# Attention rounds of a hybrid decoder kernel: exponential, turn and product put one, two and three steps behind the scores

## What is computed

```python
def swa_prompt(q, k, v, sinks):            # window attention of the prompt
    ...
    s = jnp.einsum('bnqkgd,bnskd->bnkgqs', qb, kk) * SW_HEAD_DIM ** -0.5
    ...
    p = sink_softmax(jnp.where(mask, s, NEG), sinks)
    o = jnp.einsum('bnkgqs,bnskd->bnqkgd', p, vv)

def mem_attend(cq, mk, mv, q_norm):        # memory attention, prompt and samples
    q = head_rms(cq.reshape(B, L, MEM_HEADS, MEM_HEAD_DIM), q_norm)
    s = jnp.einsum('blhd,bmhd->bhlm', q, mk.astype(F32)) * MEM_HEAD_DIM ** -0.5
    p = jax.nn.softmax(s, axis=-1)
    return jnp.einsum('bhlm,bmhd->blhd', p, mv.astype(F32)).reshape(B, L, MEM_WIDTH)
```

## Time and profile before

| | us |
|---|---|
| median of 3 runs | 3210.73 (3206.9 to 3217.41) |
| the profiled execution | 3207.76 |
| its span, first to last instruction | 3206.0 |
| TensorE busy | 2960.2 (92%) |
| VectorE, ScalarE, GpSimd busy | 1284.7, 694.7, 640.7 |
| mean granted TensorE clock | 0.938 of full |

### The profile page before, as it was taken

One profiled execution on the slowest core, in us unless ns is written; L12 is line 12 of the kernel. 1 busy time (PEld: TensorE's weight loads), 2 busy tenths in 40 slices (PEclk: granted clock), 3 DMA queues, 4 the chain that ended last, 5 costly groups with the idle time before them and its releaser, 6 DMA issues.

```text
span 3206.0 us, 42285 instructions
## 1 busy us (share of the span) xinstructions
PE 2960.2 (92%) x16482; PEld 2630.6 (82%) x16482; DVE 1284.7 (40%) x2195; ACT 694.7 (22%) x1164; POOL 640.7 (20%) x322
## 2 busy tenths in 40 slices
PE   6899999998899999999978878979789999999999
PEld 5678888887799999999966765767569999999997
DVE  4223444444444444444462223233353444444444
ACT  4321122222211111111143313333332111111110
POOL 4003232223312111221140010000023112211220
PEclk9889999999899999999988789798779999999999
DMA  4011011111111111121111210001002111211111
GB/s 157 20 53 44 25 40 47 47 34 41 40 40 46 53 39 39 40 58 39 39 47 33 73 27 14 14 14 43 14 14 60 39 39 44 54 39 39 39 46 54
DMA packets 186027, 135.37 MB, mean 42 GB/s; under 512 B 19616, under 2 KB 175456, under 8 KB 185888
## 3 DMA queue, kind: packets, MB, share of 16 engines
q1 hardware_dynamic: 181760, 129.69, 14.5%
q10 hardware_dynamic: 4160, 4.19, 0.4%
HBM read 124.61 MB, written 11.27 MB: 42 GB/s over the span
## 4 chain that ended last, share of the span: by engine, by line
PE 80%; DVE 6%; PEld 5%; ACT 4%; issue 3%; POOL 1%; PEldq 1%; DMA 0%; ACTq 0%; SPq 0%; DVEq 0%
PE ps L1366 41%; PE ps L1403 22%; PE ps L1528 3%; PEld ps L1366 3%; PE ps L1553 3%; PEld ps L1671 2%; PE ps L1538 1%; PE ps L1392 1%; PE ps L1618 1%; ACT prob L633 1%; POOL w_lo L509 1%; PE ps L1584 1%; DVE x L940 1%; ACT w_hi L505 1%; DVE normed_gained L937 1%
## 5 line engine op out<-in xcount | busy, mean ns | idle before, releaser
L937 DVE TENSOR_TENSOR x<-x,ps 128x512 f32<-128x512 f32 (+1 forms) x882 | 604.6, 686 | 919.0 <-PE ps L1403 913.7
L509 POOL TENSOR_TENSOR w_lo<-w_raw,w_hi 128x1024 fp32r<-128x1024 f32 x194 | 465.3, 2417 | 2302.6 <-ACT w_hi L505 2302.6
L1366 PE MATMUL ps<-hT_hi,w_hi 128*128 128x352 f32 x2976 | 724.7, 333 | 23.7 <-POOL w_lo L509 21.3
L1366 PE MATMUL ps<-hT_lo,w_hi 128*128 128x352 f32 x2976 | 715.4, 328 | 0.1
L1366 PE MATMUL ps<-hT_hi,w_lo 128*128 128x352 f32 x2976 | 708.6, 327 | 0.0
L1366 PEld LDWEIGHTS ps<-hT_hi,w_hi 128*128 128x128 f32 x2976 | 524.4, 192 | 61.7 <-issue 23.2
L1366 PEld LDWEIGHTS ps<-hT_lo,w_hi 128*128 128x128 f32 x2976 | 525.7, 192 | 35.3 <-issue 7.5
L1366 PEld LDWEIGHTS ps<-hT_hi,w_lo 128*128 128x128 f32 x2976 | 525.3, 191 | 26.5 <-issue 1.3
L1403 PE MATMUL ps<-w_hi,m_hi 128*128 128x512 f32 (+1 forms) x1072 | 439.9, 410 | 20.6 <-POOL w_lo L509 8.8
L1403 PE MATMUL ps<-w_lo,m_hi 128*128 128x512 f32 (+1 forms) x1072 | 432.4, 403 | 0.0
L1403 PE MATMUL ps<-w_hi,m_lo 128*128 128x512 f32 (+1 forms) x1072 | 430.8, 402 | 0.0
(11 more groups left out here) (220 smaller groups left out, 2584.5 us busy)
## 6 DMA issues: line engine op xcount, KB each, us to landing
w_raw<-in_w_ffn_in_dram SPq DMA_DIRECT2D x176, 256.0 KB, 3.2
w_raw<-in_w_ffn_out_dram SPq DMA_DIRECT2D x88, 256.0 KB, 3.7
w_raw<-in_w_in_hgrn_dram SPq DMA_DIRECT2D x52, 256.0 KB, 4.6
w_raw<-in_w_out_dram SPq DMA_DIRECT2D x32, 256.0 KB, 3.7
w_raw<-in_w_in_swa_dram SPq DMA_DIRECT2D x24, 256.0 KB, 4.1
x<-in_x_prompt_dram SPq DMA_DIRECT2D x8, 512.0 KB, 9.4
w_raw<-in_w_mem_kv_dram SPq DMA_DIRECT2D x16, 256.0 KB, 5.7
cache<-in_cache_mem_k_dram SPq DMA_DIRECT2D x4, 1024.0 KB, 7.2
```

What stands on the lines that cost most here:

```text
L509: nc.gpsimd.tensor_tensor(slot(1, s), raw[:, j3, :], slot(0, s).bitcast(F32), ALU.subtract).then_inc(w_lo, 1)
L937: return V_.tensor_tensor(out, a, b, op)
L1366: return mmul(ps[:, b0 + g, 0:TW], slot(a, s)[:, P * k:P * k + P], hT[b][:, k, TW * g:TW * g + TW], start=m < 3, stop=m >= 69)
```

## The change

ACT: the exponential moves one step back (round s-1 in step s), `prompt_hi` to the end of the step and one round forward (even steps from 4), the hook `after` goes. DVE: `prompt_lo` likewise, between the two halves of `second`, which is now called twice; the sample portions move behind the maximum. PE: each step begins with rows, turn and scores; the first filler, the sample portions, `prompt_out` of the same step's round s-3 and the second filler follow. `STEPS` goes from 20 to 19, and the projections, sums and roots for the next queries move one step forward, with 12 instead of 9 matmuls in a half. One wait is added at step 3.

```diff
--- before.py
+++ after.py
@@ -139,7 +139,7 @@
 
 B_SC, B_PT, B_RO, B_SS, B_F = 0, 2, 3, 4, 5
 
-ROUNDS, STEPS = 16, 20
+ROUNDS, STEPS = 16, 19
 S_KT, S_SSC, S_SPT, S_SPV, S_SOUT = 4, 5, 15, 17, 18
 
 INIT = 6
@@ -684,27 +684,25 @@
                                                sample_rows(rr, h2), ACT.Copy)
                 ins.then_inc(oA.sem, 1)
 
-            def pair(p, g, before, after=None):
+            def pair(p, g, before):
 
                 for s in range(STEPS):
                     before(s)
-                    if s >= 5 and s % 2:
-                        prompt_hi(p, (s - 5) // 2)
                     if s == S_SOUT:
                         sample_hi(p)
                     if s == S_SSC + NB:
                         sample_exp(p, None if g is None else col(S_SROW + g))
                     if 2 <= s < ROUNDS + 2:
                         prompt_turn(ROUNDS * p + s - 2)
-                    if s < ROUNDS:
-                        half, _, h2 = at_round(s)
-                        prompt_exp(ROUNDS * p + s, None if g is None else col(S_SINK + 3 * (2 * half + h2) + g))
+                    if 1 <= s < ROUNDS + 1:
+                        half, _, h2 = at_round(s - 1)
+                        prompt_exp(ROUNDS * p + s - 1, None if g is None else col(S_SINK + 3 * (2 * half + h2) + g))
                     if S_KT <= s < S_KT + NB:
                         sample_turn(p, s - S_KT, 2 if g is None else 1)
                     if s == S_KT + NB and g is None:
                         sample_values(p)
-                    if after:
-                        after(s)
+                    if s >= 4 and s % 2 == 0:
+                        prompt_hi(p, (s - 4) // 2)
 
             def ffn(L):
                 def split(jb, it, s, extra):
@@ -856,10 +854,10 @@
                             if g < QG - 1:
                                 if s == 11:
                                     pump.upto(n0 + 4)
-                                if s == 15:
+                                if s == 14:
                                     head_squares(u + 2, B_F)
                                     pump.upto(n0 + 5)
-                                if s == 16:
+                                if s == 15:
                                     query_std(u + 2, B_F)
                             elif s == 11:
                                 pump.upto(n0 + 4)
@@ -1121,14 +1119,10 @@
             def pair(p, g, first, second=None, s_blocks=0):
                 for s in range(STEPS):
                     first(s)
-                    if s >= 5 and s % 2:
-                        prompt_lo(p, (s - 5) // 2)
                     if s == S_SOUT:
                         sample_lo(p)
                     if s == S_SSC + NB + 1:
                         sample_scale(p, g)
-                    if s == S_SPT + 1:
-                        sample_turn(p, g)
                     if 3 <= s < ROUNDS + 3:
                         prompt_rows(ROUNDS * p + s - 3)
                     if 2 <= s < ROUNDS + 2:
@@ -1138,10 +1132,16 @@
                         prompt_max(ROUNDS * p + s, None if g is None else 3 * (2 * half + h2) + g)
                     if s == s_blocks:
                         sample_blocks()
+                    if second:
+                        second(s, 0)
+                    if s == S_SPT:
+                        sample_turn(p, g)
+                    if s >= 4 and s % 2 == 0:
+                        prompt_lo(p, (s - 4) // 2)
+                    if second:
+                        second(s, 1)
                     if s == S_SSC + NB - 1:
                         sample_max(p, g)
-                    if second:
-                        second(s)
 
             def hgrn_head(h):
                 if h == 0:
@@ -1338,17 +1338,15 @@
                             if g and s == 3:
                                 query_norm(u + 1)
                                 wait(dve, qN, u + 1, "n")
-                            if 1 <= s <= NT:
-                                add_group(G0 + 2 * s - 2, s - 1, 0)
-                            if g < QG - 1 and s == 15:
+                            if g < QG - 1 and s == 14:
                                 head_gain(u + 2, B_F, qh[:, 0, :], col(S_GQ))
                             if g < QG - 1 and s == 16:
                                 wait(dve, aE, r0 + 7, "exp")
                                 query_norm(u + 2)
 
-                        def second(s, G0=G0):
+                        def second(s, n, G0=G0):
                             if 1 <= s <= NT:
-                                add_group(G0 + 2 * s - 1, s - 1, 1)
+                                add_group(G0 + 2 * s - 2 + n, s - 1, n)
 
                         pair(2 + g, g, first, second, 3 if g else 0)
                 ffn(L)
@@ -1624,14 +1622,9 @@
 
                 for s in range(STEPS):
                     r = ROUNDS * p + s
-                    if s >= 5 and s % 2:
-                        prompt_out(r - 4)
-                    if S_SSC <= s < S_SSC + NB:
-                        sample_scores(p, s - S_SSC, window)
-                    if s == S_SPV:
-                        sample_rows_mm(p, window)
-                    fill(s, 0)
                     if 3 <= s < ROUNDS + 3:
+                        if s == 3 and p > 2:
+                            wait(pe, oV, p - 1, "7")
                         if s >= 5:
                             wait(pe, oV, p, f"{(s - 5) // 2}")
                         prompt_rows(r - 3, window)
@@ -1643,11 +1636,18 @@
                         prompt_turn(r - 2)
                     if s < ROUNDS:
                         prompt_scores(r, window)
-                    fill(s, 1)
+                    fill(s, 0)
+                    if S_SSC <= s < S_SSC + NB:
+                        sample_scores(p, s - S_SSC, window)
                     if S_KT <= s < S_KT + NB:
                         sample_keys(p, s - S_KT, 1 if window else 2)
                     if s == S_SPT:
                         sample_turn(p, window)
+                    if s == S_SPV:
+                        sample_rows_mm(p, window)
+                    if s >= 4 and s % 2 == 0:
+                        prompt_out(r - 3)
+                    fill(s, 1)
 
             def hgrn_head(h, j):
                 inc = hT_.sem
@@ -1909,14 +1909,14 @@
                             if s == 11 and z == 0:
                                 pe.wait_ge(x_added, (o + 1) * OUTG)
                                 wait(pe, qD, u + 1, "std")
-                            if 11 <= s < 15:
-                                feat(J + 2, 0, B_F, qP, (2 * (s - 11) + z, 8))
-                            if s == 15 and z == 1:
+                            if 11 <= s < 14:
+                                feat(J + 2, 0, B_F, qP, (2 * (s - 11) + z, 6))
+                            if s == 14 and z == 1:
                                 query_sums(u + 2, B_F)
-                            if s == 17 and z == 0:
+                            if s == 16 and z == 0:
                                 wait(pe, qD, u + 2, "std")
-                            if s >= 17:
-                                feat(J + 3, 1, B_F, qP, (2 * (s - 17) + z, 6))
+                            if s >= 16:
+                                feat(J + 3, 1, B_F, qP, (2 * (s - 16) + z, 6))
 
                         if g:
                             wait(pe, qN, u, "n")
```

## The result

The changed kernel takes 3089.7 us (median of 4 runs, 3087.6 to 3093.5) against 3211.4 us before: a ratio of 0.962, with a 95% interval of 0.960 to 0.964. The forecast was 3089 us. Its profiled run has a span of 3085.8 us, 120.2 us less than before.

The account below looks back on a forecast made before the run. TensorE was taken to bound the kernel, losing time in and around the five attention pairs. Gains of 18 + 18 + 31 + 31 + 24 = 122 us took 3210.7 to 3089 us; 8-in-10 range 3055 to 3150 us.

Parts of the forecast that it names:

- pair 4: Last window pair: gain 24 us; nine unfilled steps from step 10, kept at low clock, take 57 us against 62.7.
- outside the pairs: Everything outside the five attention pairs, some 2519 us: not touched by the diff, so no gain.
- The steady steps: Window-pair steps with filler: 6.3 us each; five take 31.4 us, against 40.5 in pair 3 and 45.6 in pair 4.
- signs named in advance: Trace marks of a right forecast, among them five window-pair steps in 31 to 33 us and no exp wait for the maximum.
- k_cacheT gone: In sample_scores, PE's waits for the copied transposed cache keys disappear; they were 11.0 us in eight waits of one window pair.
- The rival in which the clock stays up everywhere: Denser steps keep the clock up from step 10: 38 us more gain, 18 of it in pair 4; 3051 us; chance 0.09.
- From step 10 in pairs 2 and 3: Rest of these window pairs from step 10: 76.3 us falls to 58.4 us, gain 18 us in each.
- slower rival: Out waits for DVE's rows of the same step, 3.29 us every even step: 132 us lost, 3221 us; chance 0.06.
- The start of the window pairs: Scores(1) runs inside the w_lo chain and step 4 loses waits: gain 4 us in each of three pairs.
- Memory pairs: Pairs 0 and 1: gain 18 us each; in pair 0, 5.3 from steps 4 to 7 and 8 from steps 8 to 10.
- Wait and clock: Split of the whole gain: some 88 us from removed waits and 34 us from a higher clock.
- The 19 steps: Loop cut from twenty steps, with one more wait at step 3, already met by then: no effect.

Follow-up runs that it names:

- rows first: The changed kernel with DVE's prompt_rows moved ahead of the head gain and the sample scale: 3094.3 us, ratio 0.964.
- split first: The changed kernel with the w_lo split of step 0 moved ahead of the squares of the next head: 3091.4 us, ratio 0.963.

## Why the prediction was right

The total is right to 1 us, but its terms were not that good; the misses cancel. In us, gain forecast and measured:

| part | forecast | measured |
|---|---|---|
| pair 0 | 18 | 11.9 |
| pair 1 | 18 | 12.1 |
| pair 2 | 31 | 28.6 |
| pair 3 | 31 | 24.7 |
| pair 4 | 24 | 37.9 |
| outside the pairs | 0 | 5.0 |
| sum | 122 | 120.2 |

*The steady steps* were rebuilt well: 31.4 us for five, measured 32.6 in pairs 3 and 4; memory steps 4 to 7 21.8 us, measured 23.3. In the fed step shown above the halves of the filler cost 1.59 and 1.48 us for the 1.5 and 1.4 of the forecast, and rows 0.84 for 0.75: that is the miss of 0.2 to 0.4 us a step. The step of before was read rightly, and most signs named in advance came: k_cacheT gone, exp right behind the copy, five steps in 31 to 33 us, clock at 1.00 in the fed steps. One did not: the clock was to stay at 1.00 until the sample rows of pairs 2 and 3. In pair 3 these start at 2118 us, and the mean from 2101 to 2111 us was 0.51.

*Pair 4* is the large miss, 14 us too low. The forecast kept the low clock for its bare steps "as they hold it now"; the term that failed is this one, 57 us for the rest of the pair, measured 42 from the rows of step 10. The clock went into step 10 at 1.00, out of five steps without a wait (in the earlier trace rows they had 0.81), and it stayed there to 2220 us, past waits of 0.9 to 1.4 us. The rival in which the clock stays up everywhere was nearly right in this one place: 18 us more in pair 4, measured 14. How long it stays up is in part luck: in the kernels with rows first and with the split first it fell 74 and 80 us behind the pair's first scores, not 88, and the pair was 2 to 3 us longer.

*From step 10 in pairs 2 and 3*, 58.4 us was forecast and 67.1 us stand in pair 3 from the rows of step 10 (65.6 from its scores, above). The terms most mis-sized, from rows to rows, are step 14, which was to take 4.5 us and took 8.0, step 15 (5.2 for 3.1) and steps 11 and 16 (9.4 for 7.7 and 7.0 for 5.3); the mean clock from 2101 to 2111 us, in steps 14 to 16, was 0.51. The rows of step 14:

```profile
2094.99 1.32 DVE L1000 TENSOR_SCALAR q_heads<-ps,params 128x1056 f32<-128x1056 f32 x1 [3.94 <-ACT head_squares L541]
...
2095.98 2.35 POOL L509 TENSOR_TENSOR w_lo<-w_raw,w_hi 128x1024 fp32r<-128x1024 f32 x1 [20.49 <-ACT w_hi L505]
2096.22 2.12 DVE L935 TENSOR_TENSOR attn_stats<-attn_stats 128x1 f32<-128x1 f32 x1
...
2098.79 0.28 DVE L935 TENSOR_TENSOR attn_rows<-ps,attn_round_stats 128x128 f32<-128x128 f32 x1
...
2099.13 0.44 PE L1559 MATMUL ps<-consts,attn_rows 128*128 128x128 f32 x2 [2.49 <-DVE attn_rows L935]
```

The forecast named "out waits for DVE's rows of the same step" as the mechanism of the slower rival, and it did come, but once in a pair and not in every even step: attn_rows stood behind the head gain and a one-column add that took 2.12 us. *The start of the window pairs* gave more than the 4 us forecast. From the first scores of pair 3 to the rows of step 5, 33.5 us became 26.1. One us of it is that scores(1) cost nothing beside scores(0); the rest I haven't divided.

*Memory pairs*: steps 8 to 10 came as forecast (19.9 us for 20, 18.7 for 18.3), but steps 11 to 14 of pair 0 took 24.8 us for 20.3, longer than the 23.3 of before: the clock was low from 155 to 162 us, and the forecast had no term for that. In pair 1 steps 11 to 14 took 27.2 us, where the forecast had 25.6 less 2.8, so 22.8. The wait of out for the rows behind the reciprocal came, 2.4 us for the 3 forecast, and again the clock was low behind it (0.50 from 1765 to 1770 us), which the forecast had not priced. These two stretches are 9 of the 12 us missed here. In pair 0 the clock fell behind stretches with idle time (134.6 to 154.5 us above, busy 15.91 of 19.90), but what in it ended the full clock is not shown.

*Outside the pairs*, pair 0 starts 4.6 us earlier than before, at 94.6 us. It started between 95.0 and 98.2 us in the profiled runs of the experiments, which leave that part alone, so I take most of this for scatter, not for the change. *Wait and clock* were to share the gain 88 to 34; it is 69 to 51, and pair 4 is the main reason: 23 us of its 38 are busy time, where the forecast gave 5 us to the clock. The 19 steps cost nothing, as forecast.

So the mechanism of the waits is shown: the exponential out of the step's chain (41 us when undone, 52 alone), out ahead of the filler (63 us undone), the samples behind the filler (10 us undone). Undone one by one they cost 114 us of the 122, with overlaps between them that were not taken apart, and the first two show much of their price in the steps without filler. The first filler's new place, behind rows, turn and scores, was not undone by itself. That the total came out to 1 us is luck: 12 us too much in the memory pairs and 9 in pairs 2 and 3 stand against 14 too little in pair 4 and 5 outside the pairs.

## What to carry to other kernels

Cost a reordering of steps by the chain inside one step, but look for its gain where no filler covers the chain: with the exponential back in its own step the fed steps lost nothing, and the kernel 41 us. Do not count on where the clock falls in such a stretch: two kernels with the same waits there differed by 7 us in it. A DVE queue is a line: work moved ahead of one waiter stands behind the next, so ask who is late next before a short wait is attacked. And where a matmul uses half of the rows, put it beside its neighbour on the other half.

## What the runs showed of the hardware

Matmuls of 64 rows on different halves of the array overlap: 8 in 1.14 us, where the 4 of one half take 1.13. Issued in couples they took 19 us off this kernel in window pairs; couples in the memory pairs brought another 20, part of it by a higher clock. The Trainium skill, "TensorE: Matmul & The Clock Gate", section "The mechanism" of its part on packing small matmuls, says that tiles on different groups of rows compute side by side; the trace agrees, and the order of the instructions alone had kept this kernel from it.

A DVE instruction with two inputs was held while POOL ran its split: the add of one column took 2.12 us and ended at 2098.34, 0.01 us behind the split, and it took 1.74 us in the kernel with rows first, ending 0.02 us behind the split there. The next instruction, a reciprocal of one column, took 0.16. The Trainium skill, "SBUF — State Buffer", section "SBUF: two separate sides", says that these two engines share a pair of ports as an exclusive lock, and that a VectorE operation with two inputs in SBUF needs it; the rows agree in both kernels.

The granted clock stayed at 1.00 for 24 us of steps without filler in pair 4 of the kernel after (2195.6 to 2220.0) with TensorE busy 19.5 of the 24.4 us. In the kernel with rows first it fell in the same steps after 14 us of them (2193 to 2207), behind waits of 0.99 and 0.93 us, so the waits alone do not tell where it falls.
